# Diffusion step kernel: the conv and pool projections are moved from ahead of attention to between its units

## The reference, cut to what matters

```
h = _rmsnorm(x, g1) * (1 + sc1) + sh1
a_in, a_b, a_c, p_in, q, k, v = jnp.split(h @ w_in_l, IN_SPLITS, axis=-1)
y_attn, ctx_kv = attend(q, k, v)
y = jnp.concatenate([_short_conv(a_in, a_b, a_c, conv_l),
                     _multi_pool(p_in, pool_w_l, pool_s_l),
                     y_attn], axis=-1)
x = x + gt1 * (y @ w_out_l)
```

## Time and profile before

| | us |
|---|---|
| median of 3 runs | 3023.51 (3016.24 to 3025.56) |
| the profiled execution, its own time | 3018.63 |
| its span | 3016.6 |
| PE busy | 2875.4 (95%) |
| DVE busy | 1919.8 (64%) |
| ACT busy | 1214.3 (40%) |
| granted PE clock, mean | 0.978 |

### The profile page before, as it was taken

The page is one execution under the profiler, slowest core; times in us unless marked ns, Lnnn a source line. Parts: engine busy times, 40 slices in busy tenths (PEclk is TensorE's granted clock), DMA queues, the critical chain, the costliest instruction groups (busy, mean ns, idle before and its releaser), DMA issues.

```text
span 3016.6 us, 44946 instructions
## 1 busy us (share of the span) xinstructions
PE 2875.4 (95%) x16182; PEld 2636.8 (87%) x16182; DVE 1919.8 (64%) x4189; ACT 1214.3 (40%) x2021; POOL 25.5 (1%) x51
## 2 busy tenths in 40 slices
PE   6898999999999999999978989999999999999997
PEld 5877999999999788888867789999999998888886
DVE  3344387777875588888644445878778755555555
ACT  3343434344343444444333434443443444444443
POOL 0000000000000000000000000000000000000000
PEclk8999999999999999999988999999999999999999
DMA  7362354663856977777532124547558387666661
GB/s 276 105 238 85 122 176 127 212 208 117 260 158 222 328 285 297 280 299 283 173 117 83 43 84 147 156 133 239 181 157 259 120 291 275 230 229 212 239 219 61
DMA packets 256861, 582.51 MB, mean 193 GB/s; under 512 B 13040, under 2 KB 209904, under 8 KB 211632
## 3 DMA queue, kind: packets, MB, share of 16 engines
q1 hardware_dynamic: 251904, 546.64, 54.2%
q0 software_dynamic: 4784, 33.56, 2.8%
HBM read 476.86 MB, written 103.28 MB: 192 GB/s over the span
## 4 chain that ended last, share of the span: by engine, by line
PE 92%; DVE 3%; DMA 3%; issue 1%; ACT 1%; SPq 1%; ACTq 0%; DVEq 0%
PE ps L725 34%; PE ps L764 34%; PE ps L614 11%; PE ps L746 6%; PE ps L631 1%; PE ps L556 1%; PE ps L690 1%; DMA act_scratch<-act_h 1%; PE ps L707 1%; PE ps L660 1%; PE ps L679 1%; PE ps L578 1%; PE ps L659 1%; DMA act<-act_scratch 0%; DMA gate_scratch<-g_all 0%
## 5 line engine op out<-in xcount | busy, mean ns | idle before, releaser
L725 PE MATMUL ps<-h_lo,u_hi 128*128 128x384 f32 x2048 | 694.9, 339 | 12.8 <-ACT act_h L957 7.0
L725 PE MATMUL ps<-h_hi,u_lo 128*128 128x384 f32 x2048 | 686.2, 335 | 0.0
L725 PE MATMUL ps<-h_hi,u_hi 128*128 128x384 f32 x2048 | 685.3, 335 | 0.0
L764 PE MATMUL ps<-v_lo,w_hi 128*128 128x512 f32 x1536 | 598.6, 390 | 8.0 <-DVE v_lo L1363 5.3
L764 PE MATMUL ps<-v_hi,w_hi 128*128 128x512 f32 x1536 | 598.1, 389 | 0.0
L764 PE MATMUL ps<-v_hi,w_lo 128*128 128x512 f32 x1536 | 598.0, 389 | 0.0
L1363 DVE TENSOR_TENSOR v_lo<-wring,v_hi 128x512 fp32r<-128x512 f32 x512 | 354.1, 692 | 327.3 <-ACT v_hi L990 327.3
L990 ACT CAST v_hi<-wring 128x512 fp32r<-128x512 f32 x512 | 317.3, 621 | 554.0 <-PE ps L764 554.0
L1222 DVE TENSOR_TENSOR u_lo<-wring,u_hi 128x1024 fp32r<-128x1024 f32 x256 | 313.0, 1223 | 202.7 <-ACT u_hi L947 200.5
L725 PEld LDWEIGHTS ps<-h_lo,u_hi 128*128 128x128 f32 x2048 | 385.4, 188 | 17.5 <-DVE u_lo L1222 9.8
L725 PEld LDWEIGHTS ps<-h_hi,u_hi 128*128 128x128 f32 x2048 | 385.3, 188 | 0.0
(11 more groups left out here) (173 smaller groups left out, 3153.8 us busy)
## 6 DMA issues: line engine op xcount, KB each, us to landing
wring<-in_u_t_dram SPq DMA_DIRECT2D x128, 1024.0 KB, 5.6
wring<-in_v_t_dram SPq DMA_DIRECT2D x128, 1024.0 KB, 4.9
act_scratch<-act_h SPq DMA_DIRECT2D x256, 192.0 KB, 5.8
gate_scratch<-g_all SPq DMA_DIRECT2D x48, 1024.0 KB, 6.0
gate<-gate_scratch SPq DMA_DIRECT2D x64, 768.0 KB, 6.1
act<-act_scratch SPq DMA_DIRECT2D x64, 768.0 KB, 7.7
wring<-in_w_ada_dram SPq DMA_DIRECT2D x24, 1024.0 KB, 7.6
mod_w<-in_w_mod_dram POOLq DMA_DIRECT2D x24, 1024.0 KB, 6.6
```

The lines of the kernel that those rows point to most:

```text
L725: last = nc.tensor.matmul(ps[:, 6 + s % 2, 0:T], u[:, s % 2, k], hx[:, k], start=(k == 0 and n == 0), stop=(k == KC - 1 and n == 2))
L764: last = nc.tensor.matmul(ps[:, bank + tb], w[:, group * G + b, cols], v[:, n % 4], start=(first and n in (0, G) and k == 0), stop=(last_u ...
```

## The change

- The columns of `w_in` are reordered on the host (`IN_TILES`): queries and keys (8 blocks), values (2 tiles), and only then pooling and convolution (8 blocks, `FILL` names them).
- These last 8 blocks are no longer ahead of attention. `fill(j, third)` issues block j in thirds of 9, 9 and 6 matmuls, one third in each of attention's steps 1 to 24, between the scores of unit n+2 and T(n). They write PSUM banks 4 and 7.
- ACT copies a finished block out at steps 3, 6, ..., 24 (`fill_evac`) and splits the next weights at steps 5, 8, ..., 20. DVE makes the low parts at steps 6, 9, ..., 21 and runs the pooling and the convolution a piece at a time (`branch_step`).
- The two pooling products are issued at steps 17 and 20 (`pool_mix`), each ahead of T(17) or T(20); DVE scales them at its steps 17 and 20.
- In layer 0 the 16 modulation tiles no longer stand in attention but behind projection blocks (`ADA_AFTER`): three behind each of blocks 1, 3, 5 and 7, one behind each of 8, 9, 11 and 12. The ring's order follows: w_in, then 3 of w_ada, and so on. `w_used` rises with the first matmul that has both parts of a tile.
- The output projection takes `y` from buffers of its own, `y_hi` and `y_lo`, in the order of `PAIRS`: attention's first half, pooling, convolution, attention's second half. Its first weight block is split at step 22, its second behind the last unit. The squares of the second norm go to `sq` in place of `h`.
- POOL's stores of keys and values follow the values' copies, as before.

```
 MOD_UNIT = 32
-W_IN0 = (N_ADA1, 0)
-W_ADA2 = (W_IN0[0] + N_IN, None)
-W_OUT0 = (W_ADA2[0] + N_ADA2, N_IN)
+IN_TILES = (4, 5, 6, 7, 8, 9, 3, 0, 2, 1)
+FILL = (6, 7, 0, 1, 4, 5, 2, 3)
+N_QK, N_V = 8, 2 * TB
+N_FIRST = N_QK + N_V
+SP_FILL = N_QK + 4
+ADA_BEHIND = (3, 3, 3, 3, 2, 2, 0, 0, 0, 0)
+W_IN = (tuple(N_ADA1 + i + sum(ADA_BEHIND[:i]) for i in range(N_IN)), tuple(range(N_IN)))
+W_ADA2 = tuple(W_IN[0][i] + 1 + a for i in range(N_IN) for a in range(ADA_BEHIND[i]))
+ADA_AFTER = {1: (0, 1, 2), 3: (3, 4, 5), 5: (6, 7, 8), 7: (9, 10, 11), 8: (12,), 9: (13,), 11: (14,), 12: (15,)}
+PAIRS = ((0, 1, 2, 3), (2, 1, 0, 3), (0, 1, 2, 3))
+W_OUT0 = (N_ADA1 + N_IN + N_ADA2, N_IN)
 W_WQ0 = tuple(n + N_OUT for n in W_OUT0)
 W_SK0 = tuple(n + N_WQ for n in W_WQ0)
...
-                if M % 2:
+                if M % 2 and not (l == 0 and M < SP_FILL):
...
+                order = [2 * pair + b for pair in PAIRS[moving] for b in range(2)]
...
+                    for i, k in enumerate(order):
+                        if m == 0 and i % 2 == 0:
+
+                            pe.wait_ge(sl_rdy.sem, sl_rdy.at(l, 4 * moving + i // 2 + 1))
+                        m_hi, m_lo = (y_hi, y_lo) if moving == 1 else (h_hi, h_lo)
+                        for n, (w, hx) in enumerate(((u_hi, m_lo), (u_hi, m_hi), (u_lo, m_hi))):
                             last = nc.tensor.matmul(ps[:, m % 2, 0:T], w[:, m % 2, k], hx[:, k],
-                                                    start=(k == 0 and n == 0), stop=(k == KC - 1 and n == 2))
+                                                    start=(i == 0 and n == 0), stop=(i == KC - 1 and n == 2))
+                            if i == n == 0 and m % 2 and l == 0 and moving == 0:
+                                last.then_inc(w_used.sem, 1)
...
+            def ada_after(block):
+
+                for t in ADA_AFTER.get(block, ()) if l == 0 else ():
+                    modulation(W_ADA2[t], t, (4, 7))
+
+            column_blocks(0, N_QK, pj_mm, pj_evac, 0, after=ada_after)
...
+                                last.then_inc(w_used.sem, 1)
                     last.then_inc(pj_mm.sem, 1)
+                    ada_after(m)
...
             pe.wait_ge(poolw_ld.sem, poolw_ld.at(l, 16))
-            pe.wait_ge(vec_rdy.sem, vec_rdy.at(l, 1))
-            pe.wait_ge(pd_rdy.sem, pd_rdy.at(l, 1))
-            for b, bank in enumerate((4, 7)):
-                last = nc.tensor.matmul(ps[:, bank, 0:T], pool_blk[:, b], pool_d[:, b], start=True, stop=True)
-            last.then_inc(pool_mm.sem, 1)
-
-            pe.wait_ge(pj_evac.sem, pj_evac.at(l, 22))
+            pe.wait_ge(pj_evac.sem, pj_evac.at(l, N_FIRST))
             pe.wait_ge(cache_ld.sem, cache_ld.at(l, 32))
-            pe.wait_ge(branch_rdy.sem, branch_rdy.at(l, 1))
...
+            def fill(j, third):
+
+                if third == 0:
+                    columns_split(SP_FILL + j)
+                    pe.wait_ge(pj_evac.sem, pj_evac.at(l, N_FIRST + j - 1))
+                    if j >= 6:
+                        pe.wait_ge(pool_evac.sem, pool_evac.at(l, j - 5))
+                for k in ((0, 1, 2), (3, 4, 5), (6, 7))[third]:
+                    for n, (w, hx) in enumerate(((u_hi, h_lo), (u_hi, h_hi), (u_lo, h_hi))):
+                        last = nc.tensor.matmul(ps[:, (4, 7)[j % 2], 0:T], w[:, j % 2, k], hx[:, k],
+                                                start=(k == 0 and n == 0), stop=(k == KC - 1 and n == 2))
+                if third == 2:
+                    last.then_inc(pj_mm.sem, 1)
+
+            def pool_mix(b):
+
+                pe.wait_ge(pd_rdy.sem, pd_rdy.at(l, 1))
+                pe.wait_ge(pj_evac.sem, pj_evac.at(l, N_FIRST + 5 + b))
+                nc.tensor.matmul(ps[:, (4, 7)[b], 0:T], pool_blk[:, b], pool_d[:, b], start=True, stop=True) \
+                    .then_inc(pool_mm.sem, 1)
...
@@ -667,10 +709,14 @@
             for n in range(NU + 1):
                 if n + 2 < NU:
                     scores(n + 2)
-                if l == 0 and n < N_ADA2:
-                    modulation(W_ADA2[0] + n, n, (4, 7))
-                if l == 0 and n == ADA_TURN:
+                if l == 0 and n == 0:
                     modulation_turned(1, (4, 7))
+                if l == 0 and n == 1:
+                    pe.wait_ge(mods_rdy.sem, 2)
+                if n >= 1:
+                    fill(*divmod(n - 1, 3))
+                if n in (17, 20):
+                    pool_mix((17, 20).index(n))
                 if n < NU:
                     head, b, blocks, _ = unit(n)
...
+                if m < N_QK:
+                    columns_high(l, m + 2)
+                if m in (N_QK + TB - 1, N_FIRST - 1):
+                    M = SP_FILL - 2 if m < N_FIRST - 1 else SP_FILL
+                    columns_high(l, M)
+                    columns_high(l, M + 1)
+
+            def fill_evac(j):
+
+                act.wait_ge(pj_mm.sem, pj_mm.at(l, N_FIRST + j + 1))
+                m, src = FILL[j], ps[:, (4, 7)[j % 2], 0:T]
...
+            if l == 0:
+                act.wait_ge(w_used.sem, w_used.at(l, W_ADA2[-1] + 1))
+                for i, bank in enumerate((4, 7)):
+                    last = nc.scalar.copy(mod_raw[:, i * 4 * P:(i + 1) * 4 * P], ps[:, bank])
+                last.then_inc(ada_evac.sem, 1)
...
-                if n == 0:
-
-                    act.wait_ge(branch_rdy.sem, branch_rdy.at(l, 1))
-                    high(l, 1, y, 0)
-                    high(l, 1, y, 1)
-                if n == OUT_AHEAD:
-                    columns_high(l, SP_OUT0)
-                    columns_high(l, SP_OUT0 + 1)
...
-                if l == 0 and n == ADA_TURN:
-
-                    act.wait_ge(w_used.sem, w_used.at(l, W_ADA2[0] + N_ADA2))
-                    for i, bank in enumerate((4, 7)):
-                        last = nc.scalar.copy(mod_raw[:, i * 4 * P:(i + 1) * 4 * P], ps[:, bank])
-                    last.then_inc(ada_evac.sem, 1)
...
-                if n in (NU // 2 + 1, NU + 1):
+                if n >= 3 and n % 3 == 0:
+                    fill_evac(n // 3 - 1)
+                if n >= 5 and n % 3 == 2 and n // 3 <= 6:
+                    columns_high(l, SP_FILL + 1 + n // 3)
+                if n == NU // 2 + 1:
 
                     act.wait_ge(o_evac.sem, o_evac.at(l, n - 1))
-                    high(l, 1, y, 2 if n < NU else 3)
+                    high(l, 1, y, 2)
+                if n == NU - 2:
+                    columns_high(l, SP_OUT0)
+                    act.wait_ge(branch_rdy.sem, branch_rdy.at(l, 1))
+                    high(l, 1, y, 1)
+                if n == NU + 1:
+                    columns_high(l, SP_OUT0 + 1)
+                    act.wait_ge(branch_rdy.sem, branch_rdy.at(l, 2))
+                    high(l, 1, y, 0)
+                    act.wait_ge(o_evac.sem, o_evac.at(l, NU))
+                    high(l, 1, y, 3)
...
+            for M in range(2, SP_FILL + 2):
                 columns_low(M)
...
+            def branch_step(n):
+
+                if n == 7:
+                    dve.wait_ge(pj_evac.sem, pj_evac.at(l, N_FIRST + 2))
+                    pool_c.then(V.tensor_tensor(pool_s[:, :, 1:PW], pool_in[:, :, 0:PW - 1], pool_in[:, :, 1:PW],
...
+                if n in (17, 20):
+                    b = (17, 20).index(n)
+                    dve.wait_ge(pool_mm.sem, pool_mm.at(l, b + 1))
+                    last = V.tensor_scalar(y[:, 2 + b], ps[:, (4, 7)[b], 0:T], vecs[:, ROW_PS + b:ROW_PS + b + 1], None,
+                                           ALU.mult)
+                    last.then_inc(pool_evac.sem, 1)
+                    if b == 1:
+                        dve.wait_ge(pool_evac.sem, pool_evac.at(l, 2))
+                        dve.sem_inc(branch_rdy.sem, 1)
+                if n == 19:
+                    dve.wait_ge(pj_evac.sem, pj_evac.at(l, N_FIRST + 6))
+                    conv_c.then(V.tensor_tensor(conv_u[:], branch[:, 4:6], branch[:, 0:2], ALU.mult))
+                if n == 21:
+                    for b in range(2):
+                        last = V.tensor_scalar(y[:, b], conv_u[:, b], tap(1, b), None, ALU.mult)
+                    conv_c.then(last)
+                if n in (22, 23):
...
+                if n == 24:
+                    conv_c.close()
+                    dve.wait_ge(pj_evac.sem, pj_evac.at(l, N_FIRST + KC))
+                    V.tensor_tensor(y[:, 0:2], y[:, 0:2], branch[:, 2:4], ALU.mult).then_inc(branch_rdy.sem, 1)
...
-                if l == 0 and n == ADA_TURN + 2:
+                if l == 0 and n == 0:
                     modulation(1, (4, 7), SC2, ROW_G2)
-                if n == 2:
-                    low(1, y, 0)
-                    low(1, y, 1)
-                if n == NU // 2 + 2:
-                    low(1, y, 2)
-                if n == OUT_AHEAD:
-                    columns_low(SP_OUT0)
-                    columns_low(SP_OUT0 + 1)
...
+                branch_step(n)
+                if n >= 6 and n % 3 == 0 and n <= 21:
```

(9 more changed lines are left out.)

170 lines of the change are left out of this document (77 added, 93 removed).

## The result

The change made the kernel a little slower: 3028.36 us (median of 15 runs, 3021.21 to 3034.08) against 3019.03 for the kernel before (median of 15, 3013.75 to 3025.56). The ratio is 1.0028, 95% interval 1.0020 to 1.0037, so 6 to 11 us more. The forecast was 10.5 us less, with 3002 to 3025 as its range. The profiled execution took 3029.23 us, its span is 3027.3, 10.7 more than the span before.

What follows compares the result with a forecast made beforehand. PE, busy for 95% of the span, was taken as the bound, with room only in its waits and clock. Gains of 10.2 - 0.5 + 0.8 = 10.5 us from 3023.5 gave 3013.0 us, range 3002 to 3025.

Steps and rivals of the forecast that it cites:

- Inside the steps: Attention's steps: PE's other work of some 6.8 us covers added ACT and DVE chains of some 4.6; cost nothing.
- rival (a): Splits in attention's steps stand exposed because ACT's and DVE's queues do not clear: slower, 3039 us, chance 0.08.
- The pooling products: Steps 17 and 20: PE idles while DVE scales after each pooling product; 1.8 us each, 3.6 per layer.
- The start: Start of attention: PE waits 0.45 us for the last copy and 1.55 before T(0); 2.0 in layer 1, 2.3 in layer 0.
- the end: Steps 22, 23 and handover to the output projection: waits of 2.2, 0.7, 0.35 and 0.95 us, sum 4.2 per layer.
- No wait is longer than the 2.32 us after which the clock stayed full, so I take no clock loss: Attention's waits: clock loss taken as none; with one, each layer would lose some 1.7 to 3.4 us more.
- 20.0 us lost in layer 1: Layer 1's attention stretch in the kernel before: 72.3 us taken, 52.3 needed.
- the need of 52.3: Attention stretch before the change: 24 units (46.8 us), two pooling products (1.3) and one output block (4.16).
- forecast gain of 10.2: Layer 1's attention stretch: new waits of 9.8 us set against the 20.0 lost before.
- They fill one gap ... 3.8 against 4.6. Gain 0.8: Layer 0's projections: modulation fills the gap between keys and values, saving 4.6 us; new ring waits cost 3.8.
- Layer 0, loss 0.5 and gain 0.8: Layer 0: attention has waits of 10.1 us against 9.6 lost before, loss 0.5; projections gain 0.8.
- Rival (b): Half clock after waits in both layers, and ring costs of 2 us a round: gain 1.5, time 3022, chance 0.42.

Runs made afterwards that it cites:

- e13: The change with the edits of e1 and e2, first output block's low part later, unit 0's scores earlier, unread products in three norm waits: 2983.74 us, ratio 0.9883.
- e1: The change with DVE's scaling of the pooled blocks moved from units 17 and 20 to 18 and 21: 3021.36 us, ratio 1.0013.
- the second look at the kernel before: One more profiled execution of the kernel before, nothing changed: attention stretches of 81.4 us in layer 0 and 72.1 in layer 1.
- e12: The kernel before without the second modulation's 16 tiles, short products of constants in their place: 3007.06 us, ratio 0.9966.
- e2: The change with two modulation tiles, not three, behind each of the first four input tiles, and four behind the two value tiles: 3017.10 us, ratio 0.9992.
- e4: The change plus 20 unread products in layer 1's wait for the second value tile: 3026.61 us, ratio 1.0029.
- e15: The change with the unread products of e4 and more in three norm waits, no wait taken away: 3016.45 us, ratio 0.9997.

## Why the prediction was wrong

**The starting point** was 3023.5 us, the median of the three runs shown; fifteen runs have 3019.0. By luck this made the miss in time smaller: 15.4 us against the forecast of 3013.0, but 19.8 in the difference, 10.5 less forecast and 9.3 more measured.

**What bounds the kernel: right.** PE's waits and its clock are the room; e13 took 44 us out of the change with no product fewer.

**"Inside the steps", cost nothing: right.** No wait at steps 6 to 16, and rival (a) did not come.

**"The pooling products", 2 x 1.8 us per layer: right** in place, cause and size (1.62 and 1.87; in e1 neither is there).

**"The start", 2.0, and "the end", 4.2: right**, with 0.5 + 1.3 and 2.6 + 0.35 + 0.85; the 0.7 at step 23 did not come, and T(22) waited 0.4 longer. The idle time of layer 1's stretch is 9.1 for 9.8, of layer 0's 9.5 for 10.1.

**"No wait is longer than the 2.32 us after which the clock stayed full, so I take no clock loss": wrong.** It is the step that failed in the units. One wait that left the clock alone said nothing on others. In the second look at the kernel before, the same wait of 2.32 us was followed by half clock 1 to 2 us later:

```profile
1677.22 0.55 PE L679 MATMUL ps<-cst,pr 128*128 128x128 f32 x3 [2.32 <-DVE pr L1203]
...
1679.58 0.90 PE L679 MATMUL ps<-cst,pr 128*128 128x128 f32 x3
```

In the change, half clock followed a wait of 1.32 at the start, behind the 3.85 of the value gap, and one of 2.56 at T(22); in e1 one of 2.24. The waits of 1.62 and 1.87 at T(17) and T(20) never brought it. Of the 6.0 us by which layer 1's stretch missed, the clock is 5.1 and the need counted too low 1.7, with 0.7 less idle. The text had priced the clock (1.7 to 3.4 per layer) and then put it into a rival.

Also wrong was the side of the kernel before. Of its 20.0 us lost in layer 1, 10.0 were idle time (72.28 - 62.26) and 10.0 a busy PE. In layer 0 of e12, at full clock, PE was busy for 55.8 with the same work, the turned modulation (1.1) and the products of constants (2.0), so for 52.7 without them. By this estimate the need of 52.3 was right and some 9.5 of the 10.0 are the clock. I set all 20.0 against 9.8 of waits alone. Idle time against idle time it was 10.0 against 9.8: the forecast gain of 10.2 was to come from the clock, and the step that took the new clock loss as nothing carried it. Measured, idle time fell by 1.0 us and busy time (less the 33.3 moved in) by 3.2. Nor did the wait of 1.98 in the earlier trace rows bring the half clock behind it: PE was slow before that wait, with 1.22 for a product of 256 columns that takes 0.70 or less at full clock:

```profile
1644.49 1.22 PE L660 MATMUL ps<-kT,qT 64*128 64x256 f32 x2
```

**"They fill one gap ... 3.8 against 4.6. Gain 0.8": wrong.** This term is the larger one: layer 0's projections took 81.3 us for 72.0. PE was idle for 11.6 where the sum had 7.65 (3.8 and the 3.85 between the value groups), because in rounds 2 and 4 the tile took 6.8 and 7.4 us from request to split and not 4.8; the other 5.4 are more busy time, at a clock of 0.90. The round was costed as 7.3 us of latency against 7.2 us of work, that is, without any slack, with a median for a landing that shares the engines with three others. That the ring's slot could be given back a modulation sooner (e2: 10.9 us) I did not see.

**Layer 0, loss 0.5 and gain 0.8: wrong**, and with it the idea that the modulation only changes its place. By the medians it costs 10.3 us among the units and 20.5 in the projections.

The rule of the Trainium skill that I weighed ("SBUF — State Buffer", "A bandwidth-pool intuition that's wrong", 358 GB/s per core) gave an estimate of 11.7 us a round. Rounds 1 and 3 took 11.9 and 11.7 (requests at 54.36, 66.21, 81.62, 93.30), but a round without that bound needs as much, 2 x 4.16 + 3 x 1.01 = 11.4; round 2 took 15.4. e2 moved 20.6 MB there in 65.7 us, at 314 GB/s on average, where the change moved 22.8 in 81.3, at 280, so the change's average was at no bound. Neither average is above the rule's figure; only the earlier trace rows has more.

**Rivals.** Rival (b) named the mechanism (clock and 2 us a round in the ring) and ended at 3022, 0.42 likely; what came was (b) with more of both. A case of slower by the clock and the ring, not only by exposed splits, was missing, so the range ended too low.

Open stays why e4's gain in layer 1 does not show in its median, and what decides whether half clock follows a wait and how far it reaches: the 1.64 us at T(0) in layer 0 brought it in the change and not in e15.

## What to carry to other kernels

An order that fills waits must be checked for what sits behind the last wait it leaves: an engine that waits for a product in the middle of its queue costs more than the product, and moving that one wait a step later was worth 4.5 us here, where the reorder itself won nothing. A prefetch ring is costed from the release of the slot to the landing under load, and wants slack of more than a tenth of a microsecond: asking a modulation earlier was the main part of an edit worth 10.9 us. Compare idle time with idle time and clock with clock: a loss that is half clock does not go because waits go. Count a wait of TensorE at its length plus the half clock that may come behind it; the length of one wait that did no harm in one execution is no bound. Where a wait can't be removed, work that nobody reads can fill it, if its length is measured first; it won 9.4 us in the change and nothing clear in the kernel before.
